# Softmax probabilities transposed by DMA transfers instead of by TensorE

## The reference, cut to what matters

```python
def one_block(qblk):                       # 128 queries
    s = einsum('bqhd,bkhd->bhqk', qblk, k) * scale
    p = softmax(s, axis=-1).astype(v.dtype)
    return einsum('bhqk,bkhd->bqhd', p, v)
y_a = block_attention(qf, k, v) * silu(g_a)      # 8 heads, head width 128 (+64 rotary)
```

## Time and profile before

| | us |
|---|---|
| median of 3 runs | 5659.98 (5658.15 to 5669.94) |
| the profiled execution's own time | 5710.22 |
| its span, core 2, the slowest | 5709.2 |
| attention stage, layer 0 group 0 | about 690 to 1232 |
| attention stage, layer 0 group 1 | about 2378 to 2572 |
| attention stage, layer 1 group 0 | about 3425 to 3970 |
| attention stage, layer 1 group 1 | about 5094 to 5290 |

### The profile page before, as it was taken

How to read it: one execution, slowest core, us unless ns; L and a number is a source line. 1 busy time by engine, 2 the same in 40 slices (tenths; PEclk the granted TensorE clock), 3 DMA queues, 4 the chain that set the end, 5 groups by cost and what they waited for, 6 DMA issues and landing times.

```text
span 5709.2 us, 69371 instructions; the slowest of 8 cores (5649.3 to 5709.2 us)
## 1 busy us (share of the span) xinstructions
PE 5200.3 (91%) x25228; PEld 2424.7 (42%) x25228; DVE 2173.7 (38%) x3195; ACT 1199.0 (21%) x1909; POOL 569.7 (10%) x1070
## 2 busy tenths in 40 slices
PE   4888999989999996899999899998999987789998
PEld 2344444434444443344444444443444433334443
DVE  1332655642222144452234465455222224445223
ACT  2111333321111111222212133333111112122111
POOL 1100000001110000111210000000101000011120
PEclk7889999989999998999999999998999998899998
DMA  9675233237664667589985522323444455857996
GB/s 195 108 149 120 38 56 60 50 55 120 107 103 72 132 157 150 97 140 166 168 188 111 128 42 51 54 57 62 82 74 77 79 122 144 159 97 130 158 153 156
DMA packets 252032, 622.78 MB, mean 109 GB/s; under 512 B 71914, under 2 KB 98348, under 8 KB 242228
## 3 DMA queue, kind: packets, MB, share of 16 engines
q0 software_dynamic: 149696, 479.49, 50.2%
q1 hardware_dynamic: 102004, 138.86, 7.8%
HBM read 1048.88 MB, written 48.79 MB: 192 GB/s over the span
## 4 chain that ended last, share of the span: by engine, by line
PE 79%; DMA 11%; DVE 5%; issue 3%; ACT 1%; SPq 0%; DVEq 0%; POOL 0%; ACTq 0%; POOLq 0%
PE psum L195 77%; DVE arena L232 2%; PE psum L207 2%; DMA u_scr<-arena 2%; DMA arena<-u_scr 2%; DMA arena<-w_ada 1%; ACT arena L228 1%; DVE arena L254 1%; DMA arena<-scr 1%; DMA kv_o<-arena 1%; DMA arena<-x 1%; DMA arena<-w_in 1%; DMA v_scr<-arena 1%; DMA y<-arena 1%; DMA arena<-b_ada 1%
## 5 line engine op out<-in xcount | busy, mean ns | idle before, releaser
L195 PE MATMUL psum<-arena 128*128 128x512 bf16 (+4 forms) x22576 | 4840.6, 377 | 277.4 <-DMA arena<-u_scr 83.9
L195 PEld LDWEIGHTS psum<-arena 128*128 128x128 bf16 (+2 forms) x22576 | 2171.1, 100 | 2894.1 <-issue 726.2
L228 ACT ACTIVATE arena<-psum 128x512 f32<-128x512 f32 (+4 forms) x1054 | 673.0, 643 | 3438.1 <-PE psum L195 2704.5
L232 DVE TENSOR_TENSOR arena<-psum,arena 128x512 f32<-128x512 f32 (+4 forms) x728 | 490.8, 677 | 2105.0 <-PE psum L195 1946.5
L154 POOL DMA_DIRECT2D arena<-w_in x600 | 320.6, 535 | 3781.7 <-PE psum L195 3264.3
L232 DVE TENSOR_TENSOR arena<-arena 128x512 f32<-128x512 f32 (+7 forms) x738 | 553.2, 761 | 249.1 <-ACT arena L228 116.9
L254 DVE SCALAR_TENSOR_TENSOR arena<-arena,psum 128x256 bf16<-128x256 f32 (+1 forms) x192 | 124.9, 651 | 373.5 <-PE psum L195 194.5
L228 ACT ACTIVATE arena<-psum,stats 128x1280 bf16<-128x1280 f32 (+1 forms) x192 | 200.3, 1043 | 180.9 <-DVE stats L1383 131.7
L228 ACT ACTIVATE arena<-arena 128x512 f32<-128x512 f32 (+3 forms) x152 | 129.8, 873 | 434.3 <-DVE arena L232 171.6
L1383 DVE TENSOR_REDUCE stats<-psum 128x1 f32<-128x1280 f32 x128 | 189.5, 1480 | 3.0 <-PE psum L195 2.9
L232 DVE TENSOR_TENSOR arena<-cst,arena 128x2560 bf16<-128x2560 f32 x64 | 177.7, 2817 | 3.5 <-DMA arena<-dwt 3.5
(11 more groups left out here) (57 smaller groups left out, 859.9 us busy)
## 6 DMA issues: line engine op xcount, KB each, us to landing
arena<-w_in POOLq DMA_DIRECT2D x600, 512.0 KB, 7.0
arena<-w_bproj POOLq DMA_DIRECT2D x256, 256.0 KB, 7.1
arena<-w_ada POOLq DMA_DIRECT2D x96, 512.0 KB, 17.4
arena<-w_out POOLq DMA_DIRECT2D x64, 512.0 KB, 12.7
arena<-x SPq DMA_DIRECT2D x24, 1024.0 KB, 17.6
arena<-scr SPq DMA_DIRECT2D x24, 1024.0 KB, 7.1
scr<-arena SPq DMA_DIRECT2D x12, 1024.0 KB, 3.9
y<-arena SPq DMA_DIRECT2D x24, 512.0 KB
```

The costliest lines, as they stand in the source:

```text
L195: ins = self.nc.tensor.matmul(out.ap, lhsT=l.ap, rhs=r.ap, start=(i == 0), stop=(i == n - 1))
L228: self.op(self.act, reads, writes, lambda: self.nc.scalar.activation(out=out.ap, in_=in_.ap, func=func, **kw))
L232: self.op(eng, [a, b], [out], lambda: eng.h.tensor_tensor(out=out.ap, in0=a.ap, in1=b.ap, op=op))
```

## The change

`stage_t` loses its TensorE transposes and the copies out of PSUM. It issues instead, for each 128 queries, one transposing DMA on SP's queue, straight from P to `PTb` in SBUF: in group 0 one transfer of 128 by 1280 bf16 elements an item, in group 1 two of 128 by 256. The two banks that held the transposes (one in group 1) go to the ring of the projections. The order of the steps changes too: `stage_v` moves forward to 0.3 of the item's filling work, `stage_t` stands right behind `stage_n`, ahead of the last 0.4 and of the next item's scores. `per` is now the whole divided by the items plus one.

```diff
-    def dma(self, q, out, in_, reads=(), writes=()):
+    def dma(self, q, out, in_, reads=(), writes=(), transpose=False):
...
-        q.eng.h.dma_start(out=oap, in_=iap).then_inc(q.sems[s], 16)
+        if transpose:
+            q.eng.h.dma_start_transpose(out=oap, in_=iap).then_inc(q.sems[s], 16)
+        else:
+            q.eng.h.dma_start(out=oap, in_=iap).then_inc(q.sems[s], 16)
...
-            ps.use([5, 6, 7] if GEN else [3, 4, 5, 6, 7])
+            ps.use([3, 4, 5, 6, 7] if GEN else [2, 3, 4, 5, 6, 7])
             Ss = [PB(ps, 0, 3)] if GEN else [PB(ps, 0, 1), PB(ps, 1, 1)]
-            PTB = (3, 4) if GEN else (2,)
-            per = (48 * NH * 16 + 16 * NH) * MM / n_it
+            per = (48 * NH * 16 + 16 * NH) * MM / (n_it + 1)
...
             def stage_t(i):
                 P, _ = state.pop(i)
                 qi = i % GRP
-                for k8 in range(0, nkt, 8):
-                    n8 = min(8, nkt - k8)
-                    pt = PB(ps, PTB[k8 // 8], 1)
-                    cx.trs([...], identb.v())
...
-                    if k8 == 0:
-                        cx.actf(dst, ptv, AF.Copy)
-                    else:
-                        cx.op(cx.dve, [ptv], [dst], lambda: nc.vector.tensor_copy(out=dst.ap, in_=ptv.ap))
+                dv = PTb.all()
+                for q in range(NQ):
+                    c0 = (qi * NQ + q) * 128
+                    cx.dma(cx.qs, sub(dv, dv.ap[:, :, c0:c0 + 128]), sub(P, P.ap[:, q * Lk:(q + 1) * Lk]), transpose=True)
...
             for i in range(n_it):
                 stage_x(i)
-                fill.run(0.6 * per)
-                stage_n(i)
-                fill.run(0.4 * per)
+                fill.run(0.3 * per)
                 if i >= 1 and i % GRP == 0:
                     stage_v(i - 1)
+                fill.run(0.3 * per)
+                stage_n(i)
+                stage_t(i)
+                fill.run(0.4 * per)
                 if i + 1 < n_it:
                     stage_s(i + 1)
-                stage_t(i)
```

## The result

The changed kernel takes 5971.3 us (median of 4 runs) against 5660.0 us: 1.0549 times as long, with a 95% interval of 1.0527 to 1.0571. Slower, as forecast, but by 311 us and not by 90. The time lies in the stated range. Its size needs the forecast's waits together with one half of the second rival, transfers that wait for one another. Some executions, of every kernel, ran at a lower granted clock on one die; they are left out of all times and ratios here.

What follows compares the result with a forecast made beforehand. PE, busy for 91% of the span, was taken to set the time. Group 0's -36 us and group 1's +126 us gave +90 us on the 5660 us median: 5750 us, range 5565 to 6130.

Steps and rivals of the forecast that it cites:

- the forecast's waits: PE waiting for transfers ahead of V: 53 us a stage in group 0, 69 us in group 1; chance 0.38.
- the second rival: Transposing transfers run block by block and their chain sets group 0's pace: 6038 us, or near 6660; chance 0.23.
- the removed TensorE work: Transposes and waits taken off PE: 71 us a stage in group 0, 6 us in group 1.
- forecast -18 us a stage: Group 0's net: 53 us of new DMA waits less 71 us of removed transposes and waits.
- the slack of 2.9 us: Group 0: 8.1 us of PE work before V less 5.2 us until P is normalised, left for the closing transfer.
- the chain of transfers: Each transfer waits on SP for the one before; a group 0 group lasts at least 7.4 + 4T us against 28.1.
- T: Group 0's time for one transfer from issue to landing, taken as 6 us, between 3.6 and 19 us.
- the first way: Group 0's wait per group as transfer time less slack, 6 - 2.9 = 3.1 us; the chain gave 3.3 us.
- forecast +63 us a stage: Group 1's net: 69 us of new waits for two chained transfers an item, less 6 us removed.
- T': Group 1's time for one transfer from issue to landing, taken as 4.5 us, between 1.9 and 9.6 us.
- the lower bound of 3.6 us: Least landing time of a group 0 transfer, priced from other small transfers: 3.2 us plus 0.4 us for 256 more pieces.
- The first: Rival: transfers land in time and the kernel gets faster, 5584 us, or 5506 us without any wait; chance 0.31.

Runs made afterwards that it cites:

- the control: Kernel before, TensorE transposes and copies kept, V one item later in two halves of 256 queries: 5693 and 5697 us, 1.0090 of the kernel before.
- the ablation: Changed kernel with group 1's stages back on TensorE transposes and the old order, group 0 keeping the transposing DMAs: 5740 us, 1.0166 of the kernel before.
- slots_one: Changed kernel with `PTb` tracked block by block, so no transfer waits for the last, and one transfer in group 1: 5804 and 5808 us, 1.028 of the kernel before.
- after_noload: Changed kernel with branches B and C reusing one weight block, 48 of 49 loads a stage left out: 5613 to 5648 us, 0.9962 of the kernel before.

## Why the prediction was wrong in size

**Right.** The direction; that PE would wait for the transfers ahead of V in nearly every group (27 of group 0's 32); that group 1 would lose most, by two chained transfers an item; that neither the queue of SP's other loads nor late weights would matter; and, by the control, roughly the worth of the removed TensorE work.

**Group 0: forecast -18 us a stage, measured +64 and +41, by the ablation +47 each.** In the first stage the difference of 82 us has three parts. The waits for transfers came to 90 us (14 of them), not 53. The clock cost some 24 us (busy time 472 us where the kernel before, less its transposes, has 447), and I had put it at 5 us either way. The rest of the idle time fell by 15 us (38 to 113 - 90 = 23), not by 35. Over the forecast: 37 + 24 + 20 = 81.

**The step that failed is the slack of 2.9 us, and in it the chain of transfers; T was not undersized.** I took T = 6 us; all of group 0's transfers had a median of 4.65, the closing ones of the first stage 4.5 in the mean. The slack is the time from the closing transfer's issue until PE comes to V. At the 14 waits of the first stage it was -0.5 us in the median and -1.6 in the mean: PE had stopped before the closing transfer was even issued at 8 of them, and at most 1.3 us after it at 4 more. The other terms of the slack were nearly right. Of the stage's 16 closing items P was ready 4.0 to 5.7 us after the maximum's start at 12 and after 7.2 to 7.9 at 4, where DVE had the filling's operations ahead; I had 5.1, from two items of the old order. PE came to V 6.7 to 8.0 us after the maximum's start (once 9.2); I had 8.0.

What took the rest is SP's wait for the third transfer. At 10 of the 14 waits (10 of 13 in the second stage) the closing P was ready, but its transfer was issued only when the third had landed, 0.9 to 20.4 us after the normalisation, 5.4 in the mean. I had the chain as an alternative: 6 - 2.9, or a group of 7.4 + 4T against 28.1, where it counts only once T passes 5.2 us on average. In the trace it adds to the first way, and single transfers are enough. The third transfer of a group took 7.1 us in the median, beside a weight load in 15 of 16 cases, and the closing P was ready 5.4 us behind the third one. One third transfer took 24.8 us, and PE waited 21.9. A single value for T, the same at all four places, hid that. `slots_one` confirms it: without the chain the slack in that stage was 2.3 us in the median, and the waits fell from 90 to 57 us.

**Group 1: forecast +63 us a stage, measured +97 and +86, by the ablation +108 each.** Here T' was the undersized term: 5.1 us in the median of all instead of 4.5, twice an item. PE waited not 4.3 us at 16 places but 8.2 us in the mean at 12, 99 us in the first stage instead of 69 (90 in the second): at these places the first transfer of the pair took 7.2 us and the second 4.7 in the mean, and PE came to V 4.1 us after the normalisation, where I had 4.7. The other missing term is again the clock, 21 us, since slow matmuls followed all 21 waits of 5 us or more. Together they are 51 us over the forecast in the first stage; the ablation says 45 a stage.

**The cause of T was bounded, not understood.** I priced the transfer by rows of other small transfers and put the weights' traffic into group 1 alone. Without weight loads it takes 3.37 us in group 0, close to the lower bound of 3.6 us, and 2.29 us in group 1; the loads add 1.3 us in the median and far more in the tail in group 0, where the engines were busy for only 0.30 of the stage before, and 2.8 us in group 1. The tie may be one of time as well: a projection that ends on PE frees the weight buffer, and POOL's loads were issued 1.3 us and less than 1 us ahead of the slow transfers in the two places shown. In the first stage 44 of the 64 transfers had a load beside them, and among the slow third ones 15 of 16.

**The rivals.** The first (in time, faster) described what happens without weight loads. Of the second, the first half (block by block) is refuted: 1280 and 256 pieces take 3.37 and 2.29 us, so eight more blocks of 128 by 128 cost 1.1 us, 0.13 us each. By that the part that grows with the size runs at 262 KB / 1.08 us = 243 GB/s. Its other half, the wait for the last transfer, was at work, but with gaps: SP waited 48.9 us of the first stage for its own transfers, so they did not set the pace throughout. The Trainium skill, DMA: Bandwidth & Descriptors, section "Latency and other measured facts", has 261 GB/s, and the trace of `after_noload` agrees within 7%. The price of 1309 ns for one block, in the Trainium skill, VectorE: DVE Perf Modes, section "The three transpose paths", can't be multiplied by the blocks: ten of them took 3.37 us here, not 13.1. The transpose on TensorE that the prediction gives as 219 ns is 218 in the earlier trace rows; nothing hangs on it.

**Left open.** Whether a weight load and a transposing transfer in flight together share the engines packet by packet or whether the turning makes it worse was not separated. The 24.8 us transfer has no explained cause. Nor is it known how much PE would gain from missing weight loads without any transposing DMA.

## What to carry to other kernels

A wait that replaces work has to be priced with everything that its transfer waits for before it is issued, the transfer before it too, and with the tail of the latency beside the traffic that is really there, not with a mean. Give a DMA on the path of an in-order engine a whole step of the pipeline, with buffers tracked piece by piece, and PE's own wait for it all but goes (4.7 us here, with one more of 8.9 us by way of ACT); the same DMA with less than a step of slack cost 5.5% here, and gained 1.2% with a step more. Count a long TensorE wait with the slow matmuls behind it: the 7 us of waiting shown above cost about 9.

## What the runs showed of the hardware

A transposing DMA from SBUF to SBUF of 128 by 1280 bf16 lands 3.3 us after its issue with little beside it, one of 128 by 256 after 2.3 us, and SP's queue is held for 1.35 and 1.15 us by the issue. In the changed kernel, with weight loads under way, the medians were 4.65 and 5.1 us and the longest 24.8. After each of PE's 40 waits of 5 us or more inside the four stages, 5 to 13 matmuls stood 427 ns apart in place of 215; shorter waits were followed by such matmuls sometimes, one of 1.8 us in `after_noload` by 7. With a long wait in most items the granted clock of a stage fell from 0.98 to 0.84.
